# Convolution layer's projections by seven quarter products, their tiles issued from ScalarE's queue

## The reference, cut to what matters

```python
def conv_mixer(a, state, w_in, w_conv, w_out):
    gb, gc, v = jnp.split(a @ w_in, 3, axis=-1)      # 1024 -> 3 x 1024
    u = gc * v
    u_ext = jnp.concatenate([state.astype(u.dtype), u], axis=1)
    t = a.shape[1]
    conv = w_conv[0] * u_ext[:, 0:t]
    for k in range(1, CONV_WIDTH):
        conv = conv + w_conv[k] * u_ext[:, k:k + t]
    return (gb * conv) @ w_out, u_ext[:, t:]

def compress(rows, w_cmp):                           # the 8 samples' cached rows, 2048 each
    blocks = rows[:, :nc * CMP_BLOCK].reshape(b, nc, CMP_BLOCK, N_KV_HEADS, 2, HEAD_DIM)
    return jnp.einsum('bnlgcd,lgcde->bngce', blocks, w_cmp)

h = h + conv_mixer(rmsnorm(h, norm_mix[0]), ...)
h = h + (jax.nn.silu(f @ w_gate) * (f @ w_up)) @ w_down      # f = rmsnorm(h, norm_ffn[0])
```

## Time and profile before

| | |
|---|---|
| median of 3 runs | 1281.48 us (1278.38 to 1283.33) |
| the profiled execution's own time | 1278.62 us |
| its span, first to last instruction | 1276.7 us |
| TensorE busy | 1191.6 us, 93% |
| VectorE busy | 471.1 us, 37% |
| ScalarE busy | 282.0 us, 22% |
| GpSimd busy | 205.0 us, 16% |
| moved by DMA | 330.06 MB, mean 259 GB/s |
| mean granted TensorE clock | 0.979 of full speed |

### The profile page before, as it was taken

The page is one execution under the profiler, slowest core; times in us unless marked ns, Lnnn a source line. Parts: engine busy times, 40 slices in busy tenths (PEclk is TensorE's granted clock), DMA queues, the critical chain, the costliest instruction groups (busy, mean ns, idle before and its releaser), DMA issues.

```text
span 1276.7 us, 37806 instructions
## 1 busy us (share of the span) xinstructions
PE 1191.6 (93%) x15722; PEld 981.8 (77%) x15722; DVE 471.1 (37%) x1367; ACT 282.0 (22%) x757; POOL 205.0 (16%) x344
## 2 busy tenths in 40 slices
PE   7999999999999998998786879989899999999998
PEld 5887886999999976675344547787878977878976
DVE  2110114677774332003757674233211311212213
ACT  1000003110010022134867763121010110110122
POOL 3022132021340000223444541010000000000000
PEclk9999999999999998998989899999999999999999
DMA  9786869998443374564556876499999999989831
GB/s 308 294 321 244 316 242 336 152 392 306 139 159 116 149 280 149 169 105 132 182 178 222 263 232 237 158 387 385 399 363 379 360 360 379 349 341 380 318 124 37
DMA packets 109644, 330.06 MB, mean 259 GB/s; under 512 B 15816, under 2 KB 34201, under 8 KB 107812
## 3 DMA queue, kind: packets, MB, share of 16 engines
q1 hardware_dynamic: 91156, 263.86, 56.5%
q0 software_dynamic: 17168, 63.50, 16.3%
q10 hardware_dynamic: 1152, 0.30, 0.1%
HBM read 319.16 MB, written 15.70 MB: 262 GB/s over the span
## 4 chain that ended last, share of the span: by engine, by line
PE 86%; DVE 5%; issue 3%; ACT 2%; DMA 2%; POOLq 0%; POOL 0%; ACTq 0%; DVEq 0%
PE bank L1975 20%; PE bank L2591 15%; PE bank L2077 12%; PE pbank L2602 6%; PE bank L2113 6%; PE bank L2031 5%; PE pbank L2591 3%; PE bank L2602 3%; PE bank L2181 2%; DMA gring<-in_moe 1%; PE bank L2543 1%; PE bank L2208 1%; PE bank L2348 1%; PE bank L2303 1%; PE pbank L2543 1%
## 5 line engine op out<-in xcount | busy, mean ns | idle before, releaser
L2591 PE MATMUL bank<-X,gring 128*64 128x96 f32 x4608 | 197.0, 247 | 5.5 <-issue 5.5
L2591 PEld LDWEIGHTS bank<-X,gring 128*64 128x64 f32 x4608 | 193.0, 138 | 10.1 <-issue 10.1
L1975 PE MATMUL bank<-aT,gring 128*128 128x288 f32 x768 | 193.0, 410 | 3.5 <-DVE aT L1306 3.5
L1975 PEld LDWEIGHTS bank<-aT,gring 128*128 128x128 f32 x768 | 146.6, 192 | 46.2 <-issue 5.6
L2602 PE MATMUL pbank<-Q,X 128*32 128x256 f32 x1152 | 75.3, 379 | 0.0
L2077 PE MATMUL bank<-aT,gring 128*128 128x144 f32 x528 | 72.0, 286 | 0.0
L2031 PE MATMUL bank<-Q,X 128*64 128x64 f32 x2048 | 63.3, 223 | 7.7 <-issue 7.7
L2031 PEld LDWEIGHTS bank<-Q,X 128*64 128x64 f32 x2048 | 61.3, 138 | 11.7 <-issue 11.3
L1901 DVE TENSOR_TENSOR X<-X,bank 128x96 f32<-128x96 f32 x72 | 18.4, 256 | 134.5 <-ACT X L1252 132.6
L2077 PEld LDWEIGHTS bank<-aT,gring 128*128 128x128 f32 x528 | 67.7, 190 | 0.0
L1894 DVE TENSOR_TENSOR hT<-hT,bank 128x288 f32<-128x288 f32 x48 | 18.9, 448 | 128.5 <-PE bank L2543 128.5
(11 more groups left out here) (387 smaller groups left out, 1779.3 us busy)
## 6 DMA issues: line engine op xcount, KB each, us to landing
gring<-in_moe SPq DMA_DIRECT2D x176, 512.0 KB, 5.9
Q<-in_moe SPq DMA_DIRECT2D x72, 512.0 KB, 7.1
gring<-in_dense_gu SPq DMA_DIRECT2D x44, 512.0 KB, 14.1
Q<-in_cache_cmp POOLq DMA_DIRECT2D x64, 256.0 KB, 5.6
Q<-in_cache_cmp SPq DMA_DIRECT2D x64, 256.0 KB, 5.3
gring<-in_conv_in SPq DMA_DIRECT2D x24, 512.0 KB, 10.8
gring<-in_dense_down SPq DMA_DIRECT2D x16, 704.0 KB, 5.4
gring<-in_ple_gate SPq DMA_DIRECT2D x16, 512.0 KB, 6.2
```

The source lines that it names most:

```text
L1975: ins = pe.matmul(bank(label, k)[:, 0:T], tile[:, 128 * i:128 * i + 128], rhs[:, i, :], start=i == 0, stop=i == C - 1)
L2591: ins = pe.matmul(m_bank(i, M_GU + f)[64 * w:64 * w + 64, CAP * u:CAP * u + CAP], gslot(("m", 0), 2 * f + u)[:, o:o + 64], ae[:, c, :], st ...
```

## The change

1. **Pairs by seven products.** The 24 input and 8 output tiles of the convolution become 16 pairs (`CI` = 12 and `CO` = 4), computed by the dense layer's scheme, now `pair_product(n, x, s)`. The pairs of channels c, c+1 (c even) are: `gc` and `v` of c, `gc` and `v` of c+1, `gb` of c and c+1; then the output tiles two by two. The dense pairs follow with numbers 16 to 37. Results are `("ha", n)` and `("hb", n)`, tiles `("w", k)`.
2. **VectorE** makes the weight sums and token sums of these pairs (the sums lie in `tS`, `sample`, `pT_`, `tmp_`, `wr_`, buffers that are filled with their own data later), splits the normalization in halves with token sums between, and puts the products together: `pair_out` for the input pairs, `pair_added` for the output pairs, `gated` for the convolution.
3. **Loads.** SP issues the first 11 tiles, all its pages and `wc`, and then nothing else until the dense tiles from number 41. Tiles 11 to 40 are issued by ScalarE, two after each `first_product(n)`. POOL's first pages wait for tile 1. POOL's loads for the later stages wait for pair 15.
4. **`compress`** comes behind the pairs of `COMPRESS_AFTER`: 4, 5, 7, 8, 10, 11, 12, 13.
5. **The stage's end.** `css` and `ct` stand ahead of pair 15; then `bv`, two tables, the norm's sum, four tables. The first dense pair starts when four chunks are normalized.

```diff
+CI, CO = 12, 4
+DN = CI + CO
+WN = DN + HALVES * FC
+COMPRESS_AFTER = {4: 0, 5: 1, 7: 2, 8: 3, 10: 4, 11: 5, 12: 6, 13: 7}
...
+        def pair_loads(eng, first, last):
+
+            for k in range(first, last):
+                n = k // 2
+                if n < CI:
+                    c = 2 * (n // 3) + (n % 3 == 1)
+                    src = A["conv_in"][3 * c + k % 2] if n % 3 < 2 else A["conv_in"][3 * (c + k % 2) + 2]
+                elif n < DN:
+                    src = A["conv_out"][k - 2 * CI]
+                else:
+                    src = A["dense_gu"][(k - 2 * DN) // (2 * FC), (k - 2 * DN) % (2 * FC)]
+                load_tile(eng, ("w", k), src)
...
         @block.sync
-            for c in range(3):
-                conv_loads(c)
+            pair_loads(sp, 0, GS)
...
-            conv_loads(3)
             early_pages(1)
             for b in range(1, B):
                 late_pages(b)
                 if b + 1 < B:
                     early_pages(b + 1)
-                if b + 3 < C:
-                    conv_loads(b + 3)
-                elif b < B - 1:
-                    for c in range(3 * (b - 5), 3 * (b - 5) + 3):
-                        g_load(("co", c), A["conv_out"][c])
...
+            pair_loads(sp, 2 * DN + GS - 2, 2 * WN)
...
         @block.gpsimd
             pool.wait_ge(ptab_in, 16)
+            g_arrived(pool, ("w", 1))
             early_pages(0)
...
+            full(pool, ("hb", DN - 1))
             pool.memset(rout, 0.0).then_inc(lt_clear, 1)
...
         @block.scalar
+            for n in range(DN):
+                if n == DN - 1:
+                    for a in range(2):
+                        rstd(kcscale[a], bank(("css", a))[:, :], ("css", a))
+                first_product(n)
+                if n:
+                    pair_loads(act, 2 * n + GS - 2, 2 * n + GS)
+                if n > CI:
+                    for c in range(2 * (n - CI) - 2, 2 * (n - CI)):
+                        norm_square(1, c)
+                if n in COMPRESS_AFTER:
+                    compressed(COMPRESS_AFTER[n])
...
         @block.vector
+            dve.wait_ge(first_in, 16 * NFIRST)
+            for k in range(4):
+                weight_sum(0, k)
+            normalized_halves(0, 0)
+            for k in range(4):
+                weight_sum(1, k)
...
+            for n in range(CI):
+                c = 2 * (n // 3) + n % 3
+                pair_out(n, sg[:, 0, :], sg[:, 1, :], True)
+                settled()
+                drained(dve, ("hb", n))
+                if n % 3 < 2:
+                    gated(c)
+                else:
+                    for i in range(2):
+                        dve.tensor_tensor(zT[:, c - 2 + i, :], sg[:, i, :], tmp[:, i, :], ALU.mult).then_inc(z_ready, 1)
...
         @block.tensor
-            for c in range(C):
-                for name in ("gc", "v", "gb"):
-                    g_linear((name, c), aT, ready=0 if c == 0 and name == "gc" else None)
-                if c >= 2:
-                    compress(c - 2)
-            for c in range(C):
...
-                g_linear(("co", c), zT)
-                if c in (2, 5):
-                    compress(B - 2 + c // 5)
...
+            for n in range(DN):
+                if n == 0:
+                    pe.wait_ge(a_ready, 4)
+                elif n == CI:
+                    pe.wait_ge(z_ready, 4)
...
+                pair_product(n, aT if n < CI else zT, n // CI)
+                if n in COMPRESS_AFTER:
+                    compress(COMPRESS_AFTER[n])
...
-            norm_of_sum(1)
             distance_bias()
             for i in range(6):
                 sample_table(i)
+                if i == 1:
+                    norm_of_sum(1)
```

More of the change, by code:

```diff
@@ new lines, in normalized_halves, with both_halves @@
+            def normalized_halves(i, s):
+                scaled_by(("norm", i))
+                for c in range(4):
+                    normalized(i, c)
+                dve.wait_ge(a_ready, C * i + 4)
+                token_sum(s, 0, aT)
+                for c in range(4, C):
+                    normalized(i, c)
+                dve.wait_ge(a_ready, C * i + C)
+                for k in range(1, 4):
+                    token_sum(s, k, aT)
+            def both_halves(t):
+                return t.unsqueeze(1).to_broadcast([128, 2, HT])
@@ new lines, in two, with pair_sums @@
+            def two(t):
+                return t.rearrange("p (s t) -> p s t", s=2)
+            def pair_sums(n, following):
+                a, part, u = bank(("ha", n)), part_of(n), conv_u2 if n < DN else u2
+                full(dve, ("ha", n))
+                dve.wait_ge(p1_copied, n + 1)
+                chain(dve.tensor_tensor(u, part[:, 0:HT], a[:, 2 * HT:3 * HT], ALU.add))
+                if following:
+                    weight_sum(n + 2, 0)
+                settled()
+                chain(dve.tensor_tensor(two(part[:, HT:3 * HT]), both_halves(u), two(a[:, 0:2 * HT]), ALU.add))
+                if following:
+                    weight_sum(n + 2, 1)
+                settled()
@@ new lines, in pair_out @@
+            def pair_out(n, gate, up, following):
+                a, b, part = bank(("ha", n)), bank(("hb", n)), part_of(n)
+                u3 = part[:, 2 * HT:3 * HT]
+                pair_sums(n, following)
+                drain(dve.tensor_tensor(up[:, HT:T], u3, a[:, 0:HT], ALU.add), ("ha", n))
+                full(dve, ("hb", n))
+                chain(dve.tensor_tensor(up[:, 0:HT], u3, b[:, 2 * HT:3 * HT], ALU.add))
+                drain(dve.tensor_tensor(gate, part[:, 0:2 * HT], b[:, 0:2 * HT], ALU.add), ("hb", n))
+                if following:
+                    weight_sum(n + 2, 2)
+                    weight_sum(n + 2, 3)
@@ L1419, in dense_hidden @@
                 settled()
-                chain(dve.tensor_tensor(two(part[:, HT:3 * HT]), both_halves(u2), two(a[:, 0:2 * HT]), ALU.add))
-                if n + 2 < FT:
-                    weight_sum(n + 2, 1)
+                drain(dve.tensor_tensor(up[:, HT:T], up[:, HT:T], a[:, 0:HT], ALU.add), ("ha", n))
+                full(dve, ("hb", n))
+                chain(dve.tensor_tensor(up[:, 0:HT], up[:, 0:HT], b[:, 2 * HT:3 * HT], ALU.add))
                 settled()
-                drain(dve.tensor_tensor(up[:, HT:T], u3, a[:, 0:HT], ALU.add), ("fa", n))
@@ L1425, in dense_hidden @@
-                full(dve, ("fb", n))
-                chain(dve.tensor_tensor(up[:, 0:HT], u3, b[:, 2 * HT:3 * HT], ALU.add))
-                drain(dve.tensor_tensor(tmp[:, 0, :], part[:, 0:2 * HT], b[:, 0:2 * HT], ALU.add), ("fb", n))
-                if n + 2 < FT:
+                drained(dve, ("ha", n))
+                drain(dve.tensor_tensor(gate, gate, b[:, 0:2 * HT], ALU.add), ("hb", n))
+                if following:
                     weight_sum(n + 2, 2)
                     weight_sum(n + 2, 3)
+            for n in range(CI, DN):
+                pair_added(n, n < DN - 1)
+                if n == DN - 2:
+                    for c in range(1, 4):
+                        add_squares(1, c)
@@ L1431, in dense_hidden @@
+            for c in range(4, C - 1):
+                add_squares(1, c)
+            normalized_halves(1, 2)
+            for k in range(4):
+                weight_sum(DN + 1, k)
+            sample_tables()
+            compressed_keys()
+            def dense_hidden(n):
+                up = tmp[:, 1, :]
+                pair_out(DN + n, tmp[:, 0, :], up, n + 2 < FT)
                 s = sg[:, n % 2, :]
@@ L2137, in dense @@
                 pe.wait_ge(a_ready, ready)
-                for n in range(FT):
-                    dense_hidden(n)
+                for n in range(DN, WN):
+                    pair_product(n, aT, 2)
                 for j in range(C // 2):
```

338 lines of the change are left out of this document (156 added, 182 removed).

## The result

| | before | changed |
|---|---|---|
| median, four runs each on the same chip | 1279.93 us (1276.64 to 1283.33) | 1310.41 us (1308.8 to 1315.02) |
| ratio to before, 95% interval | | 1.0244 [1.0205, 1.0283] |
| the profiled execution's own time, its span | 1278.62, 1276.7 us | 1315.02, 1313.3 us |
| mean granted clock | 0.979 | 0.963 |
| VectorE busy | 471.1 us | 540.2 us |

The account below looks back on a forecast made before the run. TensorE was taken to bound the kernel (86% of the chain), with page loads hidden by only 1 to 2 us. Terms 1.4 + 5 - 21.2 + 23.2 + 5.7 + 6 = +20 us gave 1301.5 us, range 1281 to 1317.

Parts of the forecast that it names:

- start of the stage to first `compress`, TensorE and VectorE: VectorE's normalizations and token sums delay the first products by 2.3 us; the first `compress` starts 1.4 us later.
- wait for `w_cmp`: Before the first `compress`: 4.2 MB of tiles ahead of or beside `w_cmp` delay it, +5 us.
- TensorE's work saved between first and last start: From first to last `compress` start, TensorE's own work falls from 143.6 to 122.4 us, -21.2.
- five waits for pages: In the five one-pair gaps between `compress`, late pages make TensorE wait 4.6 us each, +23.2 (bounds 14.5 and 30).
- from the last `compress` to the dense layer: From the last `compress` start to the first dense product, 34.0 us in place of 28.2, +5.7.
- all come first: Case for `w_cmp`, before the first `compress`: all eight tiles precede it, making the wait 5.9 us.
- landing at up to 12 us. I take 11.5: In one-pair gaps, ScalarE's tiles delay pages; they land 11.5 us after their buffer's release, a 4.6 us wait.
- all seven landings lie between 9.75 and 10.8 us: Kernel before: late pages land this long after their buffer's release, just inside the 11.84 us of projections.
- The clock: TensorE's clock halves after idle waits before `compress`: 1 us for each of six, +6 (bounds 0 and 12).
- only the bare waits: Rival, chance 0.22: tiles fit beside the pages, `w_cmp` is in time, the clock holds; +2.4 us, 1284.
- Pages in time: Rival, chance 0.08: pages land 6.86 us after release and TensorE's saving stands; -14 us, 1267.
- Everything collides: Rival, chance 0.12: landing 12.9 after release, `w_cmp` 8 us late, clock lost each time; +36 us, 1317.

Follow-up runs that it names:

- experiment 1: Changed kernel, but SP issues tiles 11 to 40 behind `w_cmp` and each sample's pages, and ScalarE issues none: 1290.13 us, ratio 1.0083.
- experiment 9: Kernel before, with only its convolution tiles from the tenth on issued by ScalarE, three after each `gc`: 1296.57 us, ratio 1.0109.
- experiment 5: Changed kernel with only three page halves loaded once, the other page loads of samples 1 to 7 left out: 1272.06 us, ratio 0.9929.
- experiment 2: Changed kernel with the `compress` starts spread evenly, 9 to 11 quarter products apart, ScalarE still issuing the tiles: 1303.35 us, ratio 1.0175.
- experiment 3: Changed kernel with two edits, tiles issued by SP behind the pages and `compress` starts spread evenly: 1283.24 us, ratio 1.0018.
- experiment 4: Changed kernel with 20 needless matmuls of 144 columns before each of the five `compress` that wait for pages: 1308.56 us, ratio 1.0213.
- experiment 7: Changed kernel without page loads of samples 1 to 7, and with SP issuing the tiles behind `w_cmp`: 1264.19 us, ratio 0.9874.
- experiment 8: Changed kernel, tiles on SP, `compress` starts 9 to 13 products apart, the last after pair 15, norm's sum and tables behind it: 1272.12 us, ratio 0.9938.

## Why the prediction was right, and where it was off

The direction and the chain of causes held, and the number lies in the range: 1310.4 us measured, 1301.5 forecast, 1281 to 1317 given. That it lies in the range is in part luck. `w_cmp`, the page waits and the clock all came dearer than forecast, and a gain that was not forecast, 8.6 us of pauses that went from `compress`, made up for a part. Without it the time would have been 1319. The sum by its terms, forecast and measured in the two traces:

| step | forecast | measured |
|---|---|---|
| start of the stage to first `compress`, TensorE and VectorE | +1.4 | +2.0 |
| wait for `w_cmp` | +5 | +9.8 |
| TensorE's work saved between first and last start | -21.2 | -19.9 |
| five waits for pages | +23.2 | +31.6 |
| from the last `compress` to the dense layer | +5.7 | +6.5 |
| clock, less the pauses that went from `compress`, up to the last start | +6 | +4.1 |
| after the dense layer's start | 0 | +2.5 |
| sum | +20 | +36.6 |

- **Start.** VectorE before the first products, as forecast: waits of 2.90 and 1.2 us, and the five pairs end at 53.03 (52.5 said).
- **`w_cmp` was mis-sized.** The step was 4.2 MB at 413 GB/s, "10 us: 58", of which I took 5 us of wait. It landed at 62.8, 14.7 us later than before. The larger part of the error is the amount of data. The count of eight tiles has ScalarE's of pairs 1 to 3; those of pair 4, asked for at 47.2 and 47.6, come first too, since all eight of ScalarE's have landed by 60.1. With SP's two that makes ten tiles, 5.2 MB, or 12.7 us at 413 GB/s: 60.8. The other 2 us are the rate. 413 is that of the earlier trace rows alone; from 24 to 48 us the changed kernel moved 345 and 313 GB/s with the engines 104 to 105% busy, and over all the time up to the landing 348, the kernel before 342. The bound of 5.9 for "all come first" left out the same two tiles, so it was no bound. That ScalarE's tiles are the cause is shown by experiments 1 and 9; experiment 5 shows that later pages are not.
- **Work saved.** A pair took 6.96 to 7.06 us, 6.86 said: nine pairs in 63.0 us.
- **Page waits were mis-sized.** All five stood where they were said to stand, before batches 1, 3, 5, 6 and 7 and not before 2 and 4. But the step "landing at up to 12 us. I take 11.5" was low: `compress` starts 11.9 to 14.1 us after the release, waits of 6.3 us on the mean. The step let a third of ScalarE's 1.05 MB fit into idle DMA time. In the trace the tiles are not fitted in. From 75 to 76 us ScalarE's queue moves 0.35 MB and SP's 0.04; the tile asked for at 73.5 lands in 3.8 us, while SP's page of 76.3 takes 9.3. With the tiles behind the pages the same page took 5.0 (experiment 1). The Trainium skill, DMA: Bandwidth & Descriptors, section Queues, rings and completion order, says that a DMA engine serves the queues in turn. The trace agrees from 78 to 80 us, where the queues of SP, POOL and ScalarE move 0.26, 0.25 and 0.23 MB, and shows no such even turn from 75 to 76. The reading that all seven landings lie between 9.75 and 10.8 us took POOL's pages alone; SP's for sample 7 came after 11.3, so the slack before the change was as small as 0.5 us.
- **End.** +6.5, of 5.7 said; the first dense product starts at 257.0, where 243 was forecast, by the sum of what is above. The reorder of norm and tables was costed at nothing and is worth nothing within 1 us.
- **The clock** was a true term with a covered size. The six `compress` behind a wait took 58.57 us, 12.85 over 6 x 7.62. That is above the upper bound of 12. To go half way because the waits are "mostly shorter" failed, as `compress(5)`, behind the shortest wait (4.8 us), took 9.85 us, as much as the others. The Trainium skill, TensorE: Matmul & The Clock Gate, section HAM oscillation, had it right: every wait was followed by the slow clock, six times in six. What brought the row down to 4.1 is the gain I did not forecast: the pauses in `compress`, 9.5 us in all eight before (70.5 - 61.0 us), are under 1 us in all after. (Of the clock's 12.85 us and of the 8.6 us of this gain, 2.3 and 2.1 fall to the last `compress` and stand in the row of the end.)
- **Later.** In the profiled execution the dense stage holds a pause of 3.48 us at 273.25 that none of the other traces with these products has in its chain (those of experiments 1 to 5 and 7 have x1216 records there unbroken). That is part of why the traces differ by 36.6 us and the medians by 30.5. A wait of 1.2 us for VectorE's token sums, at 260.39, is in this row too.

The rivals: "only the bare waits" is out, since the tiles did not fit beside the pages and the clock did not hold. "Pages in time" needed a landing 6.86 us after the release and got 11.7 at best; experiment 7 shows what TensorE's saving is worth then, 9.5 us by the medians' ratios (14 forecast). "Everything collides" took landing at 12.9, `w_cmp` 8 us late and the clock lost each time; the parts read 13.4, 9.8 and six times in six. In its mechanism that was the case that came, at the size of the profiled trace (+36), and its chance of 0.12 looks too low: I had given to separate cases what has one cause, since here the same tiles delayed `w_cmp` and pages alike, and the clock fell at each of these delays.

## What to carry to other kernels

Before work that covers a load is made shorter, measure the load's whole turnaround, from the release of its buffer to its last landing on any queue, and compare it with the new gap: here 9.7 to 11.3 us under 11.84 was free, and over 6.86 it took back more than the products saved. Moving loads onto an idle engine's queue is not free bandwidth: it changes who comes first. Ask for bulk loads behind those that TensorE waits for; in experiment 2 some 4 us later was enough. When several suspected costs hang on one resource, they may well come together, so their upper ends belong into one case. And read a wait that the view puts under "issue" against the landings: in experiments 1, 3 and 9 six of them were waits for a page.

## What the runs showed that was not expected

- **The pauses inside `compress` stand behind a load of instructions.** In the kernel before they are 7.7 us in 7, with the page loads left out 1.5 us in 2, in experiment 3 13.2 us in 8. The profile gives them no releaser, but it records the loads of queue q8, "instruction", 16 KB each. All 41 pauses over 0.3 us inside `compress`, over the traces of all eleven kernels, end 1.2 to 1.6 us after such a record ends, and so does the pause of 3.48 us at 273.25 (1.4). In experiment 3 the record ends at 96.87 and TensorE goes on at 98.24. That TensorE waits for its next instructions there is the plain reading, though no run changed these loads. It also fits that the pauses go with DMA traffic: in the kernel before the DMA engines were 101 to 106% busy in the 2 us ahead of the four such loads looked at. Page loads are not needed for it: experiment 7 has none that lands after 58 us and still 4.0 us in 4; ahead of the last three of these loads the engines were 78 to 86% busy, with the tiles.
- **Full DMA engines do not mean one rate.** At 104% busy the changed kernel moved 313 GB/s from 36 to 48 us, and the kernel before 413 GB/s from 40 to 50 at 101%, but only 279 from 24 to 36 at 107%. What sets the rate stays open.
- **A half clock cost about the same after each wait:** 1.84 to 2.32 us per `compress` over 7.62, after waits of 4.8 to 9.8 us. The clock also fell behind shorter pauses, of 2.4 us in experiment 4, 2.6 in experiment 8 and 1.9 in experiment 9; in experiment 3 it held over pauses of up to 2.2 us.
